# Score operands stored ready by head, low parts on the vector engine, panel loads one tile earlier

## The reference

```
xn   = rmsnorm(x) * w                         # [1056, 1024]
proj = xn @ w_in                              # q, k, v, forget, z, xBC, dt, gates
q, k = rmsnorm per head (64 wide) * q_w, k_w  # 16 heads
s    = q.k / 8 + (cum_logf[t] - cum_logf[s]);  p = softmax(s, causal);  att = p @ v
xBC -> causal convolution, SiLU -> chunked state-space scan, gated by silu(z), grouped rmsnorm
x   += (sigmoid(g_att) * (att @ w_pa) + sigmoid(g_ssm) * (ssm @ w_pb)) @ w_out
x   += relu(rmsnorm(x) @ w_up)^2 @ w_down
```

## Time and profile before

| | us |
|---|---|
| median of three runs | 2888.79 |
| profiled execution | 2885.89 |
| its span | 2884.1 |
| PE busy | 2737.1 (95%) |
| DVE, ACT, POOL busy | 1577.2, 1022.4, 405.7 |
| projection, from first to last matmul | 41.3 to 378.5 |
| attention with z and xBC | 378.5 to 1317 |

### The profile page before, as it was taken

One profiled execution on the slowest core, in us unless ns is written; L12 is line 12 of the kernel. 1 busy time (PEld: TensorE's weight loads), 2 busy tenths in 40 slices (PEclk: granted clock), 3 DMA queues, 4 the chain that ended last, 5 costly groups with the idle time before them and its releaser, 6 DMA issues. The chain is left out here.

```text
span 2884.1 us, 47789 instructions
## 1 busy us (share of the span) xinstructions
PE 2737.1 (95%) x18754; PEld 2658.0 (92%) x18754; DVE 1577.2 (55%) x2867; ACT 1022.4 (35%) x2353; POOL 405.7 (14%) x475
## 2 busy tenths in 40 slices
PE   6998979999999999997999989998989999999999
PEld 5997978989999889887999979998989999999999
DVE  4336337656566565565898864464373444434434
ACT  4223336556666655653434331121231111111110
POOL 0000012212122222222555520000000000000000
PEclk8999999999999999998999999999989999999999
DMA  3222232132232222215888873343221111111112
GB/s 115 90 90 53 79 90 91 43 101 76 67 108 76 66 93 58 84 63 140 205 194 214 201 203 121 112 134 128 65 99 58 45 44 45 44 45 44 48 67 96
DMA packets 334448, 273.31 MB, mean 95 GB/s; under 512 B 95952, under 2 KB 311632, under 8 KB 334096
## 3 DMA queue, kind: packets, MB, share of 16 engines
q1 hardware_dynamic: 334224, 270.25, 32.9%
HBM read 197.90 MB, written 72.28 MB: 94 GB/s over the span
## 5 line engine op out<-in xcount | busy, mean ns | idle before, releaser
L411 PE MATMUL banks<-w_hi,xn_hi 128*128 128x256 f32 x1440 | 407.8, 287 | 8.7 <-DVEq L368 5.0
L411 PE MATMUL banks<-w_lo,xn_hi 128*128 128x256 f32 x1440 | 405.5, 286 | 0.0
L414 PE MATMUL banks<-xn_hi,w_hi 128*128 128x352 f32 x1152 | 379.5, 329 | 0.7 <-ACT att_xs L986 0.7
L414 PE MATMUL banks<-xn_hi,w_lo 128*128 128x352 f32 x1152 | 378.7, 329 | 0.0
L414 PE MATMUL banks<-xn_lo,w_hi 128*128 128x352 f32 x1152 | 378.2, 328 | 0.0
L411 PE MATMUL banks<-w_hi,xn_lo 128*128 128x256 f32 x1280 | 366.3, 286 | 0.0
L411 PEld LDWEIGHTS banks<-w_hi,xn_hi 128*128 128x128 f32 x1440 | 276.7, 192 | 10.6 <-DVEq L368 5.1
L411 PEld LDWEIGHTS banks<-w_lo,xn_hi 128*128 128x128 f32 x1440 | 276.6, 192 | 0.2
L1704 PE MATMUL banks<-h_hi,w_hi 128*128 128x352 f32 x768 | 248.8, 324 | 1.9 <-DVEq L1625 1.9
L1704 PE MATMUL banks<-h_lo,w_hi 128*128 128x352 f32 x768 | 248.6, 324 | 0.0
L1704 PE MATMUL banks<-mlp_uhi,w_hi 128*128 128x352 f32 x768 | 248.6, 324 | 0.0
(11 more groups left out here) (293 smaller groups left out, 6160.8 us busy)
## 6 DMA issues: line engine op xcount, KB each, us to landing
w_raw<-in_w_in SPq DMA_DIRECT2D x44, 1024.0 KB, 5.5
scratch_xbc<-att_co SPq DMA_DIRECT2D x32, 512.0 KB, 2.6
ssd_ab<-scratch_acum SPq DMA_DIRECT2D x64, 256.0 KB, 6.0
br_g<-scratch_gates SPq DMA_DIRECT2D x72, 176.0 KB, 2.8
scratch_gates<-hand_tanh SPq DMA_DIRECT2D x48, 176.0 KB, 5.4
scratch_z<-att_z_stage SPq DMA_DIRECT2D x64, 128.0 KB, 1.9
ssd_xbc<-scratch_xbc SPq DMA_DIRECT2D x64, 128.0 KB, 3.4
ssd_xbc<-scratch_xbc SPq DMA_DIRECT2D x128, 64.0 KB, 3.7
```

What stands on the lines that cost most here:

```text
L411: ins = self.nc.tensor.matmul(self.bank(n, P, PW), x[:, k, t * P:(t + 1) * P], w[:, k, :], start=first, stop=end)
L414: ins = self.nc.tensor.matmul(self.bank(n, P, TT), w[:, k, m * P:(m + 1) * P], x[:, k, r * TT:(r + 1) * TT], start=first, stop=end)
```

## The change

Queries and keys are now transposed, split and stored in the form in which the scores read them while the projection runs, two heads at a time, and attention loads them; it has no preparation of its own. The q and k weights are folded in: the query weight (times 1/8) as a scale for each partition, as the rows are transposed. Squares are kept for one tile only, so ACT's square of a tile waits for DVE's sum of the one before. The transposed groups share bank 4 and are made in the step of tile n by PE, in that of tile n+1 by ACT, DVE and SP. The cached keys go the same way in steps 0 to 3 of the first round. Beside attention the stream has three banks, its low parts are DVE's, and POOL has no program. In every stream SP loads the next raw panel at tile index 4, not 5.

```diff
 class Stream:  def sp(self, sp, i, n, last):
-        if t == 5:
+        if t == 4:
             self.load(sp, i, j + 2, last)
 class HeadNormTm:
+    GROUPS, CACHED, B_TURNED = 5, 4, 4
+    def groups(self, i, n):
+        out = []
+        if i == 0 and 0 <= n < self.CACHED:
+            out.append((n, None))
+        for g in range(self.GROUPS):
+            for k in self.ended(n - 4 - g):
+                out.append((self.CACHED + (i * self.per + k) * self.GROUPS + g, (k, g)))
+        return out
     def act(self, act, i, n):
...
             s.wait_full(act, i, n)
             s.nc.scalar.activation(self.stage[x][0:m, t, :], s.bank(n, m, PW), ACT.Copy).then_inc(self.copied, 1)
-            s.nc.scalar.activation(self.sq[0:m, t, :], s.bank(n, m, PW), ACT.Square).then_inc(s.free, 1)
+            if u:
+                act.wait_ge(self.summed, u)
+            s.nc.scalar.activation(self.sq[0:m, :], s.bank(n, m, PW), ACT.Square).then_inc(s.free, 1)
+        for c, src in self.groups(i, n - 1):
+            w = self.width(src)
+            act.wait_ge(self.turned, c + 1)
+            if c >= 2:
+                act.wait_ge(self.ops_stored[c % 2], self.landed(c - 2))
+            s.nc.scalar.activation(self.t_hi[c % 2][:, 0:w], s.core.banks[:, self.B_TURNED, 0:w], ACT.Copy,
+                                   scale=self.scale(src)).then_inc(self.hi_made, 1)
     def dve(self, dve, i, n):
-            v.tensor_reduce(self.ss[:], self.sq[:].rearrange("p t (h d) -> p (t h) d", d=HD), AX.X, ALU.add).then_inc(self.meaned, 1)
+        for k, t in s.mine(self, n):
+            s.wait_free(dve, i, n)
+            v.tensor_reduce(self.ss[k % 2][0:m, t * self.HEADS:(t + 1) * self.HEADS], self.sq[0:m, :].rearrange("p (h d) -> p h d", d=HD),
+                            AX.X, ALU.add).then_inc(self.summed, 1)
+        for c, src in self.groups(i, n - 1):
+            dve.wait_ge(self.hi_made, c + 1)
+            v.scalar_tensor_tensor(out=lo, in0=bank, scalar=self.scale(src), in1=hi, op0=ALU.mult, op1=ALU.subtract).then_inc(self.lo_made, 1)
...
+            if k % 2:
+                v.tensor_tensor(stage, stage, self.w[:, None, :].to_broadcast(every), ALU.mult).then_inc(self.weighted, 1)
+    def pe(self, pe, i, n):
+        for c, src in self.groups(i, n):
+            if src is None:
+                pe.wait_ge(self.cached, 16)
+            elif src[1] == 0:
+                self.wait_normed(pe, i, src[0])
+            if c:
+                pe.wait_ge(self.lo_made, c)
+            for rows, m, col in self.blocks(c, src):
+                ins = s.nc.tensor.transpose(s.core.banks[:, self.B_TURNED, col:col + m], rows, s.core.ident[0:m, 0:m])
+            ins.then_inc(self.turned, 1)
     def sp(self, sp, i, n):
+        for c, src in self.groups(i, n - 1):
+            sp.wait_ge(self.lo_made, c + 1)
+...
 project_qkv, tensor:
                     stream.pe(pe, i, n)
+                    norm.pe(pe, i, n)
 attention_z_xbc:
-        stream.low_on_pool = True
-    B_SCORES, B_TURNED, B_PREP, B_OUT, B_TILES = 0, 2, 4, 5, (6, 7)
+    B_SCORES, B_TURNED, B_OUT, B_TILES = 0, 2, 5, (4, 6, 7)
+            def load_ops(h, g):
+                for b in range(2):
+                    sp.dma_start(first[b * HD:(b + 1) * HD, :], k_ops[h, 0:HD, cols]).then_inc(loaded, 16)
+                sp.dma_start(second[0:KX, :], k_ops[h, HD:HD + KX, cols]).then_inc(loaded, 16)
...
-                for g in prepared(h, u, 1):
-                    prep(h + 1, g)
```

More of the change, by code:

```diff
@@ L464 @@
     HEADS = PW // HD
-    def __init__(self, sb, sem, per, weights, to):
-        self.per, self.weights, self.to = per, weights, to
-        self.stage = [sb(f"norm_stage{x}", [P, NT + 1, PW]) for x in range(2)]
[L469 to L473, removed]
+    GROUPS = 5
@@ new lines, in blocks @@
+    def blocks(self, c, src):
+        if src is None:
+            rows = self.stage[1][:].rearrange("p t n -> p (t n)")
+            return [(rows[:, t * D + (2 * c + b) * P:t * D + (2 * c + b + 1) * P], P, (2 * b + t) * P) for b in range(2) for t in range(2)]
+        k, g = src
+        stage = self.stage[k % 2]
+        if g == 4:
+            return [(stage[0:TS, NT, b * P:(b + 1) * P], TS, b * TS) for b in range(2)]
+        return [(stage[:, 4 * (g % 2) + t, g // 2 * P:(g // 2 + 1) * P], P, t * P) for t in range(4)]
@@ new lines, in places, with width @@
+    def places(self, i, c, src):
+        if src is None:
+            return [(4 * c + 2 * b, 1, slice(TP, TP + PAST), b * PAST) for b in range(2)]
+        k, g = src
+        head = (i * (self.per // 2) + k // 2) * self.HEADS
+        first = 0 if k % 2 == 0 else PAST
+        if g == 4:
+            return [(head + 2 * b, k % 2, slice(TP + first, TP + first + TS), b * TS) for b in range(2)]
+        return [(head + g // 2 * 2, k % 2, slice(g % 2 * 512, (g % 2 + 1) * 512), 0)]
+    def width(self, src):
+        return 2 * TS if src is not None and src[1] == 4 else 512
@@ new lines, in sp @@
+        for c, src in self.groups(i, n - 1):
+            sp.wait_ge(self.lo_made, c + 1)
+            for head, x, cols, col in self.places(i, c, src):
+                at = (HD, 0) if x == 0 else (0, HD)
+                w = cols.stop - cols.start
+                for part, buf in zip(at, (self.t_hi, self.t_lo)):
+                    for b in range(2):
+                        sp.dma_start(self.ops[x][head + b, part:part + HD, cols],
+                                     buf[c % 2][b * HD:(b + 1) * HD, col:col + w].bitcast(F32)).then_inc(self.ops_stored[c % 2], 16)
@@ L538, in finish @@
     def finish(self, sp):
-        for x in range(2):
-            sp.wait_ge(self.stored[x], 32 * (self.stream.rounds * (self.per // 2) + 1))
+        count = self.CACHED + self.stream.rounds * self.per * self.GROUPS
+        sp.wait_ge(self.stored, 32 * (self.stream.rounds * self.per // 2))
+        for j in range(2):
+            sp.wait_ge(self.ops_stored[j], self.landed(count - 1 - (count - 1 - j) % 2))
 class Decays:
@@ L1897, in _ @@
             stream.start_sp(sp)
-            load(0)
-            for g in SEQ:
-                load_bias(0, g)
+            load_ops(0, K0)
+            load_ops(0, QA)
+            load_v(0)
+            for g in (K1, QB, KS):
+                load_ops(0, g)
             for n in range(FIRST):
@@ L2287, in _ @@
                     invert(hn, nxt[1])
-                for g in prepared(h, u, 2):
-                    make_lo(h + 1, g)
                 add_out(x)
```

321 lines of the change are left out of this document (113 added, 208 removed).

## The result

The changed kernel takes 2916.37 us by the median of four runs (2916.20 to 2918.37), the kernel before 2889.13 in the same measurement: ratio 1.0099, 95% interval 1.0081 to 1.0116. It is slower by 27 us, nearly five times the bound of 5.8 us for telling a change from none. The forecast was 2893. By its own terms, 2880 to 2905, it missed by 11 us; the result lies within the range of 2864 to 2921 only because that was drawn out to rival two at 2917. The size is that rival's and its mechanism is not what happened, so that the range holds the number is luck.

The account below looks back on a forecast made before the run. PE was taken as the bound, busy for 2737 of 2884 us. Projection +72.5, attention -68 and other stages 0 gave +4.5 on the profiled 2885.9, 2890.4; with 2.9 to the median, 2893 us; range 2864 to 2921.

Parts of the forecast that it names:

- rival two: Attention: low parts on DVE come ahead of the reciprocal that ACT's scaling waits for; +28.5 us, 2917; chance 0.25.
- attention, preparations and start: Attention: 80 operand preparations leave PE, 36 us (30 to 45); waits and clock at its start go, 5 (0 to 7).
- attention, waits: PE's 38.8 us of waits for ACT in attention: 24 gone, 5 added, 8 of clock regained; 27 us gained.
- projection, transposes: Projection: PE gains transposes of cached keys and prompt rows, 17.3 us, and 8 small pairs, 2; sum 19 (17 to 23).
- clock in the projection: Projection: PE's granted clock falls after added waits, 0.5 us for each of 15; 8 us (0 to 22).
- waits, round two, start: Projection: 15 added PE waits, 34 us; decays' transposes later in round two, 5; first loads, 2.5; stores against ACT's buffers, 1.
- end of stage: Projection's end: SP issues 8 group stores at 0.42 us ahead of v's last store, which everything waits for; 3 us.
- The wait that the change adds: Projection: PE's transposes wait for copy, square, high part and low part of the group before; 15 x 2.25 = 34 us (28 to 40).
- Cause (1): Attention: raw panel loaded at tile 4, not 5, ends ACT's waits for it; all 9.9 us of idle PE gone.
- Cause (3): Attention: POOL's low parts slow DVE, a convolution step taking 2.34 us beside them and 1.32 by the median.
- Cause (2): Attention: `make_hi`, 0.58 us, no longer stands on ACT between exponential and scaling; the size of ten waits of 0.5 to 0.9.
- Rival three: Projection: k groups' stores wait behind the 1 MB panel load on SP's queue, making ACT late; +11 us, 2904; chance 0.05.

Follow-up runs that it names:

- order kernel: From the changed kernel: on ACT and DVE, the groups' high and low parts put ahead of the tile's own copy, square and sum; 2867.97 us, ratio 0.9932.
- the filler: From the changed kernel: 16 unused matmuls of 256 columns on PE ahead of each of 19 waits for a low part; 2894.58 us, ratio 1.0025.

## Why the prediction was right in its steps and short in its sum

| step | forecast | measured |
|---|---|---|
| attention, preparations and start | -41 | -38.3 (loaded for prepared, rest as before; last of the three, -49.2) |
| attention, waits | -27 | -25.1 (the two other edits on top; made first, -14.2) |
| projection, transposes | +19 | PE busy +47.6, together with the clock; +22.5 in the order kernel, at 0.96 |
| clock in the projection | +8 (0 to 22) | 22 by the filler; 47.6 - 22.5 = 25.1 by busy time; 16 falls of 1.50 = 24 |
| waits, round two, start | +34 +5 +2.5, stores +1 | waits 53.6 for 14.1: +39.5 |
| end of stage | +3 | 14.9 for 10.0: +4.9 |
| other stages, start of the program | 0 (-4 to +4) | +3.6, +0.3 |

**The wait that the change adds** was right in place, cause and size: 18 waits of 2.06 to 2.11 us, each ended by DVE's low part, where 15 of 2.25 were put and the first q panel of round two, with three of the 18, was taken apart. The two long ones of that panel, PE at

```profile
299.76 0.66 PE L628 MATMUL banks<-ident,qkv_norm_stage 128*128 128x128 f32 x4 [3.24 <-DVE qkv_norm_stage L611]
...
313.09 1.12 PE L628 MATMUL banks<-ident,qkv_norm_stage 128*128 128x128 f32 x4 [8.30 <-DVE qkv_turned_lo L603]
```

together replace the 10.7 us of the earlier trace rows and one of 3.39 that PE had just before, in the kernel before:

```profile
245.51 0.58 PE L411 MATMUL banks<-w_hi,xn_hi 128*128 128x256 f32 x1 [3.39 <-ACT qkv_sq L505]
```

The terms sum to 42.5, measured 39.5.

**The clock** is the step that failed. The forecast had two windows of the earlier trace rows, one fall and none, and took 0.5 us for each wait. Its own rows gave more: half of the 1.5 us that its upper bound puts for a fall is 0.75. And the rate was off: the clock fell after 16 of 18 such waits, not after one in two. Two cases were too few to take a rate from. The distance between them explains nothing: those two waits, at 404.89 and 412.61, stood 7.7 us apart, about as these do. The upper bound of 22 us, "if each one costs a fall", is what the filler measured. By the rows the balance is: forecast 4.5, clock 17.1 more (25.1 for 8), transposes 3.5 more (22.5 for 19), waits 3.0 less, end 1.9 more, start of the program 0.3, attention 4.6 less gained, other stages 3.6; together 32.5, the difference of the two spans. The time looked like rival two, but its own condition did not come: the earlier trace rows's waits fell, and the low parts on DVE gained 7.5 us instead of costing 17.

**Attention's waits** came out at the right size for partly wrong reasons. Of the 38.8 us 14.7 went where 19 net were put, and not by the causes one by one. Cause (1) alone is worth nothing, 0.7 us. Cause (3), GpSimd beside DVE, is worth 6.4 alone (convolution steps 1397 ns on average before, 1316 after). Cause (2) was not tried by itself. The preparation of the earlier trace rows reads 0.38 + 0.25 - 0.16 = 0.47 us, not the 0.42 that was counted; with the operands loaded and the rest as before PE's busy time fell by 34.8 us (883.32 to 848.49), where 32.5 were summed. Causes (1) and (3) work as factors: low parts on DVE make room for the earlier load, 0.7 us without them and 7.8 with them.

**End of stage.** v's last store was issued at 379.39 before, 0.9 us after the last matmul; now the last group's eight stores stand ahead of it:

```profile
466.36 1.09 SPq L646 DMA_DIRECT2D scratch_k_ops<-qkv_turned_hi  x2
467.49 1.24 SPq L646 DMA_DIRECT2D scratch_k_ops<-qkv_turned_lo  x2
468.76 1.24 SPq L646 DMA_DIRECT2D scratch_k_ops<-qkv_turned_hi  x2
470.04 1.24 SPq L646 DMA_DIRECT2D scratch_k_ops<-qkv_turned_lo  x2
471.39 0.52 SPq L454 DMA_DIRECT2D out_v_prompt<-qkv_v_stage  x1
```

The eight issues are those that the forecast counted, at 0.62 us where the earlier trace rows gave 0.42: 5.0 for 3.4.

**Rival three** was right in mechanism. In the changed kernel the k groups' stores, which are issued behind the panel load, land later than the q groups' (stretch 60 to 400, median us to landing); with the load at the fifth tile both are at 2.4 to 2.6.

```profile
scratch_q_ops<-qkv_turned_hi SPq DMA_DIRECT2D x24, 128.0 KB, 2.4
...
scratch_k_ops<-qkv_turned_hi SPq DMA_DIRECT2D x24, 128.0 KB, 3.4
```

It cost little in the changed kernel: two waits of PE of 1.17 us, at 146.79 and 242.43, behind ACT, which had stood 2.7 us for such stores, 2.3 us where the rival put 11 and the forecast 1. In the order kernel it is part of what is left. The rule of the Trainium skill weighed ahead (DMA: Bandwidth & Descriptors, section Queues, rings and completion order) would have each of those stores begin after the load ahead of it; the trace agrees as far as the stores issued from 89.30 to 91.85, behind the load of 88.71, release ACT only at 96.03. But the load moved one tile later did not shorten the waits, 25.0 us for 22.6 (11.4 for 8.9 in those that end with a store): the load alone does not decide.

## What to carry to other kernels

A short wait in a stage where TensorE is the bound can have two prices; read the matmul spacing right after such waits, and don't take the rate of falls from two cases. Where many are to come, put the price for all of them into the sum or the range. Order each engine's step by who waits for the result: the two groups of operations changed places, no work was saved, and that was worth 48 us. An edit that takes one late transfer away can be worth nothing until the engine that releases the next one is faster; undo such edits one by one and together before pricing them.

## What the runs showed of the hardware

- After 16 of 18 waits of TensorE of 2.06 to 2.11 us its clock stood some 3 us at the lower level (matmuls of 256 columns 0.21 us apart instead of 0.12); one such fall cost 1.50 us. Sixteen filler matmuls in the gap kept the clock: 0.96 for 0.90 over the stage, 22 us.
- A store whose destination has an outermost dimension of two ran at 50 GB/s on two of sixteen DMA engines, and its issue held SP for up to 6 us. The same bytes as two stores of 64 rows landed 2.4 to 3.4 us after their issue.
- An issue of such a 64-row store takes SP 0.62 us, a panel load of 1 MB 0.37.
- What stays open: four runs of the kernel with loaded operands and the two other edits undone ranged from 2928.89 to 2944.50 us, four of the changed kernel from 2916.20 to 2918.37. In four kernels with the same 18 waits the clock fell after 13, 15, 16 and 16 of them; no run here settled on what it hangs.
